# Moving the top-k of a PEER block, and summing every V row on TensorE, in a hybrid encoder layer

## The reference, cut to what matters

```
x = x + mixer(x)
x = x + mem_cross_attn(x, mem)              # 4 heads over 256 memory tokens
h = rmsnorm(x, g_peer)
s = scores of (h @ w_pq) against 2 x 128 sub-keys, 8 heads
sv, si = top_k(s, 16)                       # per head and side
cv, ci = top_k(all 16 x 16 sums of sv, 16)  # per head: 16 experts
eidx, gate = experts of ci, softmax(cv)     # 8 x 16 = 128 experts a token
act = gelu(h . u_tab[eidx]) * gate          # 128 dot products of length 1024
x = x + sum_k act[k] * v_tab[eidx[k]]       # 128 rows of length 1024
y = rmsnorm(x, g_final)
```

## Time and profile before

| | us |
|---|---|
| runs shown | 4180.81, 4182.08, 4184.73 (median 4182.08) |
| profiled execution, its own time | 4180.31 |
| its span, first to last instruction | 4178.5 |

### The profile page before, as it was taken

One profiled execution on the slowest core, in us unless ns is written; L12 is line 12 of the kernel. 1 busy time (PEld: TensorE's weight loads), 2 busy tenths in 40 slices (PEclk: granted clock), 3 DMA queues, 4 the chain that ended last, 5 costly groups with the idle time before them and its releaser, 6 DMA issues.

```text
span 4178.5 us, 33628 instructions
## 1 busy us (share of the span) xinstructions
PE 3527.5 (84%) x8236; PEld 1526.1 (37%) x8236; DVE 2854.5 (68%) x5860; ACT 1641.2 (39%) x4373; POOL 1718.5 (41%) x1485
## 2 busy tenths in 40 slices
PE   8999979977888888888888888888897898888677
PEld 4554444422333333333333333333333333333222
DVE  2346972368486886786795795796796787687654
ACT  4343232024344444344444444444344344344333
POOL 0001232034334454445445445445445445445555
PEclk9999999988999998999999999999999999999899
DMA  3002556199999999999999999999999999999998
GB/s 107 31 30 96 186 174 234 56 368 389 411 333 418 421 412 422 420 410 422 417 409 422 420 401 422 421 400 421 421 405 421 421 407 414 421 411 412 422 421 350
DMA packets 210645, 1462.50 MB, mean 350 GB/s; under 512 B 25616, under 2 KB 25744, under 8 KB 41872
## 3 DMA queue, kind: packets, MB, share of 16 engines
q0 software_dynamic: 194880, 1377.92, 80.5%
q1 hardware_dynamic: 15568, 82.43, 5.5%
HBM read 1424.61 MB, written 35.65 MB: 349 GB/s over the span
## 4 chain that ended last, share of the span: by engine, by line
DVE 32%; DMA 26%; PE 14%; issue 8%; POOL 5%; ACT 3%; DVEq 2%; ACTq 1%; POOLq 0%; PEldq 0%
DMA arena<-in_uv,arena 26%; DVE arena L969 13%; PE ps L1391 7%; DVE arena L926 5%; POOL arena L530 4%; PE ps L1419 3%; PE ps L1377 3%; DVE arena L985 2%; DVE arena L1055 1%; DVE arena L1052 1%; DVE arena L1057 1%; DVE arena L1004 1%; DVE arena L1014 1%; DVE arena L1005 1%; DVE arena L1044 1%
## 5 line engine op out<-in xcount | busy, mean ns | idle before, releaser
L1391 PE MATMUL ps<-arena 128*128 128x512 f32 x4400 | 2165.1, 635 | 581.3 <-ACT arena L701 576.9
L530 POOL DMA_INDIRECT arena<-in_uv,arena x1280 | 1588.2, 1241 | 1701.5 <-PE ps L1391 930.8
L969 DVE SCALAR_TENSOR_TENSOR arena<-arena 128x1024 f32<-128x1024 f32 x1280 | 1548.1, 1223 | 801.8 <-DMA arena<-in_uv,arena 782.3
L1391 PEld LDWEIGHTS ps<-arena 128*128 128x128 f32 x4400 | 835.7, 199 | 1844.5 <-ACT arena L701 1017.2
L694 ACT ACTIVATE acts<-dots 128x1 f32<-128x1 f32 x1280 | 258.6, 202 | 1796.7 <-DVE arena L969 1775.4
L1419 PE MATMUL ps<-arena 128*128 128x512 f32 x1280 | 579.6, 597 | 0.0
L701 ACT ACTIVATE arena<-ident,gated 128x128 f32<-128x128 f32 x1100 | 441.8, 402 | 81.6 <-issue 7.5
L1419 PEld LDWEIGHTS ps<-arena 128*128 128x128 f32 x1280 | 246.3, 193 | 309.2 <-issue 309.2
L1275 PE MATMUL ps<-arena 128*128 128x512 f32 (+1 forms) x768 | 278.5, 522 | 3.5 <-DVE arena L814 2.9
L985 DVE SCALAR_TENSOR_TENSOR arena<-arena,gated 128x1024 f32<-128x1024 f32 x170 | 217.7, 1281 | 0.6 <-ACT gated L696 0.6
L696 ACT ACTIVATE gated<-arena,acts 128x1 f32<-128x1 f32 x640 | 188.5, 295 | 45.1 <-issue 1.4
(11 more groups left out here) (187 smaller groups left out, 2109.2 us busy)
## 6 DMA issues: line engine op xcount, KB each, us to landing
arena<-in_items SPq DMA_DIRECT2D x32, 1024.0 KB, 5.4
arena<-in_uv,arena POOLq DMA_INDIRECT x1280
qk_scratch<-arena POOLq DMA_DIRECT2D x32, 256.0 KB, 2.7
wp_scratch<-arena POOLq DMA_DIRECT2D x32, 256.0 KB, 5.5
vo_scratch<-arena POOLq DMA_DIRECT2D x32, 256.0 KB, 2.4
arena<-qk_scratch SPq DMA_DIRECT2D x2, 4096.0 KB, 15.1
arena<-vo_scratch SPq DMA_DIRECT2D x2, 4096.0 KB, 22.1
arena<-wp_scratch SPq DMA_DIRECT2D x2, 4096.0 KB, 28.2
```

The lines of the kernel that those rows point to most:

```text
L530: g.indirect_dma_start(out=ring[r], out_offset=None, in_=a["uv"], in_offset=bass.IndirectOffsetOnAxis(ap=IDXC[:, k:k + 1], axis=0))\
L969: v.scalar_tensor_tensor(out=ring[r][:, 0:D], in0=ring[r][:, 0:D], scalar=1.0, in1=H[par], op0=ALU.mult, op1=ALU.mult, accum_out=dots[:, r ...
L1391: ins = t.matmul(ACC[par][:, half * BANK:(half + 1) * BANK], diag[r], ring[r][:, D + half * BANK:D + (half + 1) * BANK], start=False, stop ...
```

## The change

It does four things. (1) VectorE's row sums, ACCV, `merge` and their semaphores go: TensorE sums every V row, so `pick` is the same for all 128 picks on every engine, and the last pick closes the sum. (2) The top-k gets a buffer of its own, TK; `load_x1` waits for `xp_norm` and `x2_kept` (the last reads of XC) instead of the chosen indices. (3) In a steady block the six steps of a quarter stand three picks apart, from pick 69; of the fourth quarter only the first two steps stay in the walk before (picks 123, 126), the other four go into the block's own walk, at picks 1, 3, 8 and 12, with its exponential at turn 5. (4) Attention of block 1 begins at pick 23 of block 0 instead of 41, and its norm and transposes (`attend_norm`, `attend_turned`, `attend_first`) go between the steps of block 0's last quarter; block 1's top-k starts at pick 78, 2 or 3 picks apart, instead of 93, 1.4 apart. The ring keeps eight slots, at other addresses.

```diff
-DVE_FIRST, DVE_END = 2, 8
-def by_dve(group):
-    return (1, 3, 5) if DVE_FIRST <= group < DVE_END else ()
-STEADY = prepare(14, ((62, 65), (70, 73), (82, 85), (94, 97)), steps(69, 2))
+STEADY = prepare(14, ((62, 65), (75, 78), (93, 96), (111, 114)),
+                 [(69, 72, 75, 78, 81, 84), (87, 90, 93, 96, 99, 102), (105, 108, 111, 114, 117, 120), (123, 126)])
+LATE_CHOOSE = (1, 3, 8, 12)
+FINAL_SQUARES, LATE_EXP, FINAL_RSTD, FINAL_SCALE, FINAL_ROWS, FINAL_GAIN = 4, 5, 6, 7, 7, 10
 FIRST = dict(...
-             q=((66, 66), (1, 1), (9, 12), (21, 24)), choose=[[72, 72, 75, 75, 78, 78]] + steps(-8, 2)[1:])
+             q=((66, 66), (1, 2), (7, 10), (17, 20)),
+             choose=[(72, 72, 75, 75, 78, 78), (3, 5, 7, 9, 11, 13), (15, 17, 19, 21, 23, 24),
+                     (26, 28, 31, 34, 37, 40)])
-SECOND = prepare(41, ((88, 91), (95, 98), (103, 106), (111, 114)), steps(93, 1.4))
-FINAL_SQUARES, FINAL_RSTD, FINAL_SCALE, FINAL_ROWS, FINAL_GAIN = 4, 6, 6, 6, 10
+SECOND = prepare(23, ((71, 74), (84, 87), (100, 103), (115, 118)),
+                 [(78, 80, 83, 85, 88, 90), (93, 95, 98, 100, 103, 105), (108, 110, 113, 115, 118, 120), (123, 126)])
...
-        H0, XC, AC, BC = (piece(D) for _ in range(4))
+        H0, XC, AC, BC, TK = (piece(D) for _ in range(5))
-        SV, SIF, SI = XC[:, 0:64], XC[:, 64:128], XC[:, 128:192].bitcast(u32)
+        SV, SIF, SI = TK[:, 0:64], TK[:, 64:128], TK[:, 128:192].bitcast(u32)
-        CAND = AC[:, 2 * TOPK * TOPK:]
+        CAND = TK[:, 2 * TOPK * TOPK:]
...
             def load_x1(b):
                 if b >= 1:
-                    hold(idx_ready, Q * b)
+                    sp.wait_ge(xp_norm, b)
+                    hold(x2_kept, b)
...
             def gather(b, k):
-                if k >= R and on_dve(k - R):
-                    hold(row_summed, b * DVE_PICKS + dve_rank(k - R) + 1)
-                else:
-                    hold(row_used, b * PE_PICKS + (k + 1 if k < R else R + pe_rank(k - R) + 1))
+                hold(row_used, b * PICKS + k + 1)
...
             def pick(b, par, group, r, slots):            # VectorE
                 v.scalar_tensor_tensor(out=ring[r][:, 0:D], ..., accum_out=dots[:, r:r + 1]).then_inc(dot_ready, 1)
-                s = r - LAG
-                if s not in slots: return
-                ...
-                    ins = v.scalar_tensor_tensor(ACCV, rows, gated[:, s:s + 1], ACCV, ALU.mult, ALU.add)
-                ins.then_inc(row_summed, 1)
...
-            choose(0, 0, upto, FIRST, 1, Q)               # VectorE, block 0
-            attend(1, upto, SECOND)
-            choose(1, 1, upto, SECOND, 0, Q)
+            choose(0, 0, 1, upto, FIRST)
+            choose(0, 0, 2, upto, FIRST)
+            attend_norm(1, upto, SECOND)
+            top(0, Q - 1, upto, turns[0:2])
+            attend_turned(1, upto, SECOND)
+            cand(Q - 1, upto, turns[2:4])
+            expert_first(upto, turns[4])
+            expert_second(0, 0, Q - 1, upto, turns[5])
+            attend(1, upto, SECOND)
+            for q in range(Q - 1):
+                choose(1, 1, q, upto, SECOND)
+            top(1, Q - 1, upto, SECOND["choose"][Q - 1])
...
+            for b in range(1, NB):                        # VectorE, blocks 1 to 9
+                upto = walker(b, par)
                 final_diag()
+                cand(Q - 1, upto, LATE_CHOOSE[0:2])
                 upto(FINAL_RSTD)
                 final_rstd(b - 1)
+                expert_first(upto, LATE_CHOOSE[2])
                 upto(FINAL_GAIN)
                 final_gain(b - 1)
+                expert_second(b, par, Q - 1, upto, LATE_CHOOSE[3])
...
-            def merge(b, par):                            # TensorE
-                t.wait_ge(row_summed, (b + 1) * DVE_PICKS)
-                for half in range(2):
-                    ins = t.matmul(ACC[par][...], ident[:, :], ACCV[...], start=False, stop=True)
-                ins.then_inc(merged, 1)
```

More of the change, by code:

```diff
@@ L93 @@
 GROUPS = PICKS // R
-LAG = 2
 assert GROUPS * R == PICKS
-DVE_FIRST, DVE_END = 2, 8
-def by_dve(group):
-    return (1, 3, 5) if DVE_FIRST <= group < DVE_END else ()
[L105 to L124, removed]
 def prepare(first, products, choose):
@@ L258, in build @@
         dots, acts, gated = sb("dots", R), sb("acts", R), sb("gated", R)
-        ring = [GR[:, r * 2 * D:(r + 1) * 2 * D] for r in range(R - 2)]
-        ring += [GR2[:, r * 2 * D:(r + 1) * 2 * D] for r in range(2)]
+        ring = [GR[:, r * 2 * D:(r + 1) * 2 * D] for r in range(R - 1)]
+        ring.append(GR2)
         diag = [rows[:, 0:P] for rows in ring]
@@ L695, in pick @@
                 act.drain()
[L696 to L699, removed]
+                act.activation(gated[:, r:r + 1], GAT[par][:, k:k + 1], ACT.Copy, scale=acts[:, r:r + 1])
                 act.drain()
@@ L971, in pick @@
                  .then_inc(dot_ready, 1)
-                s = r - LAG
-                if s not in slots:
-                    return
-                rank = slots.index(s)
-                rows = ring[s][:, D:2 * D]
-                v.wait_ge(gated_ready, b * DVE_PICKS + (group - DVE_FIRST) * len(slots) + (rank + 1))
-                if group > DVE_FIRST or rank:
-                    v.wait_ge(row_summed, b * DVE_PICKS + (group - DVE_FIRST) * len(slots) + rank)
-                if group == DVE_FIRST and rank == 0:
-                    if b >= 1:
-                        v.wait_ge(merged, b)
-                    ins = v.tensor_scalar(ACCV, rows, gated[:, s:s + 1], None, ALU.mult)
-                else:
-                    ins = v.scalar_tensor_tensor(ACCV, rows, gated[:, s:s + 1], ACCV, ALU.mult, ALU.add)
-                ins.then_inc(row_summed, 1)
             def walk(b, par, at, end):
                 for k in range(at, end):
-                    pick(b, par, k // R, k % R, by_dve(k // R))
+                    pick(b, par, k)
             def top_sets(q):
                 src = bank(4 + q)
-                return [(j, src[:, j * NK:(j + 1) * NK], AC[:, j * NK:(j + 1) * NK]) for j in range(4)]
+                return [(j, src[:, j * NK:(j + 1) * NK], CAND[:, j * NK:(j + 1) * NK]) for j in range(4)]
             def top_first(q):
@@ L1386, in _, with pick @@
             mix_out(0)
-            def pick(n, par, r):
-                t.wait_ge(diag_ready, n + 1)
+            def pick(b, par, k):
+                r = k % R
+                t.wait_ge(diag_ready, b * PICKS + k + 1)
                 for half in range(2):
                     ins = t.matmul(ACC[par][:, half * BANK:(half + 1) * BANK], diag[r],
-                                   ring[r][:, D + half * BANK:D + (half + 1) * BANK], start=False, stop=False)
+                                   ring[r][:, D + half * BANK:D + (half + 1) * BANK], start=False,
+                                   stop=k == PICKS - 1)
                 ins.then_inc(row_used, 1)
```

240 lines of the change are left out of this document (123 added, 117 removed).

## The result

| | before | after |
|---|---|---|
| median us (runs) | 4181.44 (4179.14 to 4184.73, 4) | 4157.41 (4156.30 to 4161.38, 4) |
| ratio, 95% interval | | 0.9944, 0.9926 to 0.9961 |
| repeat (e11), beside before again | 4184.29 | 4163.25; 0.9948, 0.9935 to 0.9962 |
| profiled execution, its span | 4180.31, 4178.5 | 4158.18, 4156.4 |

The change takes 0.6% off in the first runs, 24 us, and 0.5% in the repeat, 21 us. Forecast were 4155, and - 27.5.

What follows compares the result with a forecast made beforehand. The prediction took the DMA gathers to set the pace, other engines mattering only where they make one late. Its terms, - 23.6 - 5.0 + 6.8 - 4.0 - 1.7 = - 27.5 us, gave 4155 us; 8-in-10 range 4126 to 4178.

Steps and rivals of the forecast that it cites:

- Block 0's end: Block 0's end and block 1's first picks: VectorE's work, spread over more picks, fits there; gain 23.6 us of 25.1 lost.
- the reserve: How late engines may be before DMA runs dry, in the ring of gathers: at least 4.1, at most 6.9 us.
- Block 0's beginning: Block 0, picks 3 to 41: VectorE 3.8 us over without row sums, moved attention loses 4.5; gain 5.0 us.
- TensorE's bursts: Picks 21 to 30 and 41 to 50: half products make TensorE 6.0 us late; 0.4 each, 17 bursts, cost 6.8 us.
- Three-pick spacing: Top-k steps three picks apart in steady blocks stop lateness growing; gain 0.5 us a block, 4.0 us in all.
- Late steps: Four top-k steps in a block's own picks 1 to 12: nothing on the path, cost 0.
- Queues: Loads and stores on SP, gather waits on GpSimd: same bytes and order; cost 0.
- tail: Kernel's end: merge goes from the last chain and the final squares start behind the last pick; gain 1.7 us.
- the first: Rival: steady blocks give their loss back too and TensorE's bursts cost nothing; 4122 us, chance 0.15.
- The second: Rival: block 0's loss only moves, first half still losing 9.5 us and second half 6; 4165 to 4176 us, chance 0.17.
- The third: Rival: TensorE becomes the bound in picks 21 to 50 of every block; 4216 us, deciding from 2.0 a burst, chance 0.07.
- The fourth: Rival: gather, GpSimd or weights' load ends the waits at 1140 to 1257 us, VectorE's relief unfelt; 4180 us, chance 0.04.

Runs made afterwards that it cites:

- e11: The kernel after once more, unchanged, beside the kernel before again: 4163.25 us, ratio 0.9948.
- e2: Kernel after with block 1's attention put back behind block 0's top-k, four top-k steps still in block 1's first 12 picks: 4172.49 us, ratio 0.9970.
- e3: Kernel after with block 1's attention behind block 0's top-k and all 24 of block 1's top-k steps inside block 0: 4176.01 us, ratio 0.9980.
- e4: Kernel after with the top-k steps of the steady blocks two picks apart again: 4159.87 us, ratio 0.9941.
- e10: Kernel after with 16 further waits before each dot (VectorE) and 16 before each gelu (ScalarE) of block 9: 4168.40 us.
- e1: Kernel before with one part of the change alone, TensorE summing the rows of all 128 picks and no merge: 4171.33 us, ratio 0.9969.
- e7: Kernel after with attention's half products in steady blocks four picks apart, not three, and what follows moved back: 4158.60 us, ratio 0.9935.
- e5: Kernel after with attention's half products in blocks 2 to 9's preparation before every second pick, not every third: 4167.25 us, ratio 0.9960.
- e8: Kernel after with 16 further waits, holding nothing up, before each dot of block 9 on VectorE: 4167.01 us.
- e9: Kernel after with 16 further waits before each gelu of block 9 on ScalarE, none on VectorE: 4173.53 us.

## Why the prediction was right

The sum was right to 4 to 7 us (- 24 and - 21 for - 27.5), and the mechanism too: block 0's end pays. Most tells came as named: 421 and 418 GB/s there, block 0 30.5 us shorter from its first dot to block 1's (383.9 to 353.4), steady blocks at 325 to 327 (one of the repeat's at 327.8), the clock at 1.00 in block 9's first half, and 393 GB/s between picks 26 and 42 of block 0 (372 in the repeat), where under 340 would have refuted it. One didn't: at block 0's end VectorE is as busy as before, 87% of the window for 89%. What went is the stretch in which it waited for no row. Inside the sum some terms were wrong and their errors cancelled, so its closeness is partly luck.

- *Block 0's end, - 23.6:* right. Blocks 0 and 1 without the first 64 picks gave 24.0 us (23.0 in the repeat): 28.3 in block 0, less the 4.3 by which block 1 got longer. e2 and e3 show whose doing it is: of the kernel after's lead over e3 in blocks 0 and 1, 16 to 19 us, putting the attention back costs 12 to 14, and the late steps 4.5 more. The agreement of 24 over with 25.1 lost was luck: at pick 125 it is 28 over; less the reserve of 8.0, and with the 5.1 us that VectorE waited for the score product, that is 25.
- *Block 0's beginning, - 5.0:* not there. Its first 64 picks took 175.0 before, 172.8 after and 174.3 in the repeat, and 174.0 to 176.5 in e4 to e10, which have the same code there. The moved attention costs 3.9 to 5.4 (e2: 168.9), as the 4.5 said. But VectorE's own steps, which I gave wholly to the reserve, still lose some 2: e2's picks 24 to 49 stand at 405 GB/s. I had again made the sum to the stretch's end; at pick 24 it is 12 x 2.97 + 21 x 1.14 - 21 x 2.485 = 7.4 over, not 3.8. And a wait was put at nothing: the first step moved from pick 4 to pick 3 and half its score product from turn 1 to turn 2. The step's wait for TensorE grew from 0.81 to 6.15 us, and the first 16 picks take 2.3 us longer than before. Before, then after:

```profile
871.47 0.89 DVE L1001 MAX8 arena<-ps 128x8 f32<-128x128 f32 x4 [0.81 <-PE ps L1419]
```
```profile
876.12 0.89 DVE L967 MAX8 arena<-ps 128x8 f32<-128x128 f32 x4 [6.15 <-PE ps L1412]
```

- *TensorE's bursts, + 6.8:* not there. e1 has the bursts without the rest, and its steady blocks are no longer than before; e7 wins 0.4 to 2.1 us in blocks 2 to 8 where 5.6 stood in the sum. The step that failed is the reserve, 4.1 to 6.9: e5 shows 8.0 at least, so 6.0 of lateness is inside it.
- *Three-pick spacing, - 4.0:* not there (e4), and for the reason that the prediction gave against its own rival: the stops in a steady block aren't VectorE's lateness. They are loads of instructions (e8).
- *Late steps, 0:* they cost 0.6 to 0.8 us a block. This is by subtraction: blocks 2 to 8 are 4.0 to 5.7 above e1, which has neither them nor the spacing, and bursts and spacing are worth nothing that shows. The first 16 picks of these blocks are 1.5 to 2.0 us longer than before and in e1 (42.87 and 43.04 against 41.38 and 41.09), the other 112 picks 1.1 to 1.2 shorter. "Nothing on the path" failed at a wait: at the final norm's product VectorE now waits for TensorE's row of gains in each of nine blocks. How much of the cost is this wait, and how much the steps themselves, isn't shown. The list of VectorE's waits in after has this line (us in all, times, longest us), and those of before and e1 have none like it:

```profile
DVE arena L1161 <- PE ps L1431: 22.4, 9, 4.2
```

- *Queues, 0; tail, - 1.7:* right; in the chain of waits the squares follow the last pick at once.

```profile
4145.91 2.00 PE ps L1392 x4
4147.90 0.02 issue
4147.93 1.01 ACT ps L682
```

So blocks 2 to 8 came out near the forecast, + 1.7 us (+ 3.4 in the repeat) where 14 bursts and 7 spacings make 5.6 - 3.5 = + 2.1, but for other reasons: nothing from either, and the late steps' cost, which stood at 0. That is luck. Of the 5.4 us that the profiled run misses of - 27.5, 3.3 are its later first gather.

Of the rivals, the first (steady blocks give their loss back) fell with e4. The second, that the loss only moves, was right for block 0's first 64 picks, which won nothing that shows, and wrong for its end, whose window lost 114 x (1 - 418/421.5) = 1 us and not 6. The third, TensorE as the bound, decides far from here: even e5's tighter bursts cost 0.2 to 0.4 each, a fifth of its 2.0 at most. The fourth, that VectorE's relief isn't felt, fell with e2 and e3.

## What to carry to other kernels

Add up an engine's work against the time of the picks it stands in, at the point where the excess is largest, and compare it with the reserve that the ring really has; here at least 8 us were free. Add the waits too: a piece that is moved closer to the product it needs makes its engine wait, here 6.15 us at one step and up to 4.2 at another. When a kernel is bound by DMA and its small stops won't yield to scheduling, count instructions: replacing drains by semaphore waits took seven packets off the instruction queue and made the steps shorter, together 0.4 to 0.5% of the time.

## What had not been expected of the hardware

An 8 KB packet of VectorE's instructions holds a stream of 1 MB gathers up by 1.0 us at 421 GB/s, with five or six gathers in flight; one of ScalarE's by 0.7; and the two don't add (e8, e9, e10). A packet holds 128 instructions (e8: 1024 more instructions, 8 more packets). The Trainium skill, Runtime: NRT & Kernel Launch, Instruction fetch mechanics, says that an engine streams its own instructions by DMA ahead of their use and that crossing a block costs little that isn't hidden. VectorE itself loses little by it here: it idles 1.25 us before such dots in any case. The gathers pay for it, some five times a block. The Trainium skill, DMA: Bandwidth & Descriptors, Queues, rings and completion order, has each DMA engine take turns between its queues by whole packets. e10 fits a packet that holds up one DMA engine alone, though no run here shows on which DMA engine a packet ran.
